# Attention of one layer with V held stationary on column halves, and adaLN units behind the three latent qkv products

## What is computed

```python
q, k, v = qkv_heads(h, wqkv, qn, kn)      # 16 query heads, 4 key/value heads, 64 wide; RMSNorm on q and k
# prompt: every query sees the 128 prompt keys; latent: rope, the 128 latent keys and 128 cached context keys
p = softmax(concat([q @ k.T * 64 ** -0.5, sink]))[..., :-1]
o = einsum('bkgqs,bskd->bqkgd', p, v)      # 4 query heads share one key/value head
return o.reshape(B, L, 1024) @ wo
```

## Time and profile before

| what | value |
|---|---|
| median of 3 runs | 1302.45 us (1299.8 to 1305.2) |
| the profiled execution | 1300.94 us, of which its span (first to last instruction) 1299.0 us |
| mean granted TensorE clock | 0.997 of full speed |
| busy share of the span | PE 98%, DVE 34%, ACT 25%, POOL 4% |
| DMA | 497.42 MB, mean 383 GB/s |
| layer 1: latent and prompt qkv products | 664.5 to 715.2 us |
| layer 1: attention up to the projection's first matmul | 715.2 to 761.0 us |
| layer 1: projection | 761.0 to 788.6 us |

### The profile page before, as it was taken

How to read it: one execution, slowest core, us unless ns; L and a number is a source line. 1 busy time by engine, 2 the same in 40 slices (tenths; PEclk the granted TensorE clock), 3 DMA queues, 4 the chain that set the end, 5 groups by cost and what they waited for, 6 DMA issues and landing times.

```text
span 1299.0 us, 18966 instructions
## 1 busy us (share of the span) xinstructions
PE 1267.8 (98%) x7020; PEld 709.7 (55%) x7020; DVE 440.6 (34%) x1503; ACT 324.4 (25%) x718; POOL 56.8 (4%) x86
## 2 busy tenths in 40 slices
PE   6999999999999999999999899999999999999998
PEld 3876775545545454455454578655445444544544
DVE  1696272222222222222235535422222222222223
ACT  3575331121121122112121433112212211221111
POOL 0295000000000000000000000000000000000000
PEclk9999999999999999999999999999999999999999
DMA  9987999999999999999996557699999999999994
GB/s 365 385 324 302 405 401 403 414 419 419 420 420 421 421 420 421 420 419 421 363 413 284 235 227 292 248 403 418 419 420 420 421 420 421 421 421 421 419 419 193
DMA packets 84022, 497.42 MB, mean 383 GB/s; under 512 B 10681, under 2 KB 19553, under 8 KB 27648
## 3 DMA queue, kind: packets, MB, share of 16 engines
q1 hardware_dynamic: 83392, 496.47, 93.4%
q10 hardware_dynamic: 576, 0.22, 0.1%
HBM read 493.26 MB, written 3.41 MB: 382 GB/s over the span
## 4 chain that ended last, share of the span: by engine, by line
PE 85%; DVE 6%; DMA 6%; ACT 2%; SPq 1%; issue 1%; POOL 0%; DVEq 0%; ACTq 0%
PE ps L951 34%; PE ps L983 17%; PE ps L994 9%; PE ps L922 7%; PE ps L638 4%; DVE ps L1574 3%; PE ps L730 3%; DMA ring<-in_conv_w_dram 2%; PE ps L865 2%; DMA ring<-in_ada_w_dram 2%; DMA S<-in_exp_w_up_dram 2%; PE ps L606 1%; PE ps L969 1%; PE ps L906 1%; PE ps L961 1%; SPq L403 1%
## 5 line engine op out<-in xcount | busy, mean ns | idle before, releaser
L951 PE MATMUL ps<-ring,xg 128*64 128x512 f32 x1344 | 296.8, 593 | 0.2
L951 PEld LDWEIGHTS ps<-ring,xg 128*64 128x64 f32 x1344 | 104.6, 137 | 186.8 <-issue 167.9
L951 PE MATMUL ps<-S,xg 128*64 128x512 f32 x704 | 154.8, 592 | 0.3 <-DMA S<-in_exp_w_up_dram 0.3
L983 PE MATMUL ps<-ring,W 128*64 128x512 f32 x672 | 153.5, 598 | 0.0
L1866 DVE TENSOR_TENSOR ypart<-ps,ypart 128x512 fp32r<-128x512 f32 x128 | 88.5, 691 | 179.8 <-ACT ypart L1396 179.8
L1855 DVE SCALAR_TENSOR_TENSOR vec<-silu_h,W,ps 128x256 f32<-128x256 f32 x64 | 30.8, 481 | 333.3 <-ACT silu_h L1390 333.3
L994 PEld LDWEIGHTS ps<-comb,ypart 128*128 128x128 f32 x1024 | 126.3, 190 | 18.6 <-issue 18.6
L994 PE MATMUL ps<-comb,ypart 128*128 128x256 f32 x1024 | 135.2, 285 | 0.0
L1390 ACT ACTIVATE silu_h<-ps 128x256 f32<-128x256 f32 x64 | 24.6, 385 | 407.3 <-PE ps L951 407.3
L1385 ACT ACTIVATE xg<-ps 128x384 f32<-128x384 f32 x176 | 83.3, 492 | 168.1 <-PE ps L922 168.1
L1396 ACT ACTIVATE ypart<-ps 128x512 fp32r<-128x512 f32 x128 | 76.5, 598 | 184.6 <-PE ps L983 184.6
(11 more groups left out here) (249 smaller groups left out, 1097.4 us busy)
## 6 DMA issues: line engine op xcount, KB each, us to landing
ring<-in_exp_w_gate_dram SPq DMA_DIRECT2D x86, 1024.0 KB, 15.8
ring<-in_exp_w_up_dram SPq DMA_DIRECT2D x86, 1024.0 KB, 18.4
ring<-in_exp_w_down_dram SPq DMA_DIRECT2D x86, 1024.0 KB, 18.2
S<-in_exp_w_gate_dram SPq DMA_DIRECT2D x44, 1024.0 KB, 16.2
S<-in_exp_w_up_dram SPq DMA_DIRECT2D x44, 1024.0 KB, 19.0
S<-in_exp_w_down_dram SPq DMA_DIRECT2D x44, 1024.0 KB, 18.9
ring<-in_ada_w_dram SPq DMA_DIRECT2D x26, 1024.0 KB, 21.2
S<-in_ada_w_dram SPq DMA_DIRECT2D x22, 1024.0 KB, 14.4
```

Source lines behind the costliest of these rows:

```text
L951: mm = pe.matmul(PGU[64 * b:64 * b + 64, :].rearrange("p (h f) -> p h f", h=2), xg[:, places[k][m], 64 * b:64 * b + 64], gate_up_of(w[b])[ ...
L983: mm = pe.matmul(bank[64 * b:64 * b + 64, :], hidT[:, j, 64 * b:64 * b + 64], down_of(w[b])[:, j, n * 512:(n + 1) * 512], start=(j == 0), ...
```

## The change

Three edits, all in layer 1's mixer. (The convolution's taps that run as products with diagonal matrices on PE, `conv_taps`, are in both kernels and the diff leaves them as they are.)

- The eight adaLN units that lay between the latent qkv products run behind the third of them; ACT's and DVE's order follows, and DVE finishes unit group 4 only after the latent norm and rope.
- V is the stationary operand, 64 columns wide, and the transposed probabilities of all four query heads (512 columns) move. The two turns of a pair write the two column halves of one bank, so the result comes out with the head dimension on the partitions, which is what the projection reads. So `otok`, its 16 transposes and the four copies go; `wo` is loaded in another row order by four DMAs. As the queries now lie along the free dimension of the result, the division by the row sum moves ahead of the transposes (`scaled`, on the probabilities in place).
- The order of the attention changes with it: ACT copies the context half of the latent probabilities and the results, DVE the other half; the values of two turns are made together at the end of a pair; the prompt's q and k are transposed ahead of the first turn.

```diff
         B0 = 2 * EW
         qkv = ring_f[:, B0:B0 + 3072].rearrange("p (g n) -> p g n", g=G)
-        otok = ring_f[:, B0 + 3072:B0 + 5120].rearrange("p (g n) -> p g n", g=G)
...
-        probT = W[:, 2816:3840].rearrange("p (b n) -> p b n", b=2)
+        probT = W[:, 2816:4864].rearrange("p (b k n) -> p b k n", b=2, k=2)
+        TURNED = [2 * (i + 1) if i < NKV else NKV + i + 1 for i in range(2 * NKV)]
...
                     sp.wait_ge(at_qkv, 6)
-                    sp.dma_start(wo, attn_wo[0].rearrange("(k p) n -> p k n", p=P)).then_inc(ld_wo, 16)
+                    for j in range(NKV):
+                        b = j % 2
+                        sp.dma_start(wo[HD * b:HD * b + HD, QG * (j // 2):QG * (j // 2 + 1), :],
+                                     attn_wo[0, QG * HD * j:QG * HD * (j + 1), :].rearrange("(q d) n -> d q n", d=HD)
+                                     ).then_inc(ld_wo, 16)
...
-            def project(w, x, ready, per, loaded, banks):
-
-                pe.wait_ge(loaded, 16)
+            def project(w, x, ready, per, loaded, banks, first=1, loads=1):
...
                             if b == h == 0:
-                                pe.wait_ge(ready, k // per + 1)
+                                pe.wait_ge(ready, k // per + first)
...
-                    qkv_product(1, 0)
-                    ada_products(range(EARLY, EARLY + 4), ps[2])
-                    qkv_product(1, 1)
-                    ada_products(range(EARLY + 4, EARLY + 8), ps[2])
-                    qkv_product(1, 2)
+                    for n in range(3):
+                        qkv_product(1, n)
+                    ada_products(range(EARLY, EARLY + 8), ps[2])
+                    qkv_product(0, 0)
                     ada_transposes(4, ps[2])
-                    qkv_product(0, 0)
                     qkv_product(0, 1)
...
                     def at_transposes(i):
                         nk = 1 + HEADS[i][0]
-                        pe.wait_ge(at_exp, i + 1)
-                        if i == 2:
+                        pe.wait_ge(at_on, i + 1)
+                        if i == 0:
                             pe.wait_ge(at_trc, 7)
+                        else:
+                            pe.wait_ge(at_ptc, TURNED[i - 1 if i <= NKV else i - 2])
                         for kk in range(nk):
+                            bank = ps[4 + kk] if nk == 2 else ps[4 + i % 2]
                             for q in range(QG):
-                                mm = pe.transpose(ps[4 + kk][:, q * T:(q + 1) * T],
+                                mm = pe.transpose(bank[:, q * T:(q + 1) * T],
                                                   prob[:, i % 2, q, kk * T:(kk + 1) * T], ident)
                         mm.then_inc(at_pt, 1)
 
-                    def at_values(i):
-                        g, j = HEADS[i]
+                    def at_values(m):
+                        g = HEADS[2 * m][0]
                         nk = 1 + g
-                        pe.wait_ge(at_ptc, i + 1)
-                        if i >= 1:
-                            pe.wait_ge(at_on, i)
-                        for q in range(QG):
-                            for kk in range(nk):
+                        pe.wait_ge(at_ptc, TURNED[2 * m + 1])
+                        if m >= 1:
+                            pe.wait_ge(at_otc, m)
+                        for kk in range(nk):
+                            for b in range(2):
+                                j = HEADS[2 * m + b][1]
                                 v = (qkv[:, g, (NH + NKV + j) * HD:(NH + NKV + j + 1) * HD] if kk == 0
                                      else vctx[:, j * HD:(j + 1) * HD])
-                                mm = pe.matmul(ps[6][:, q * HD:(q + 1) * HD],
-                                               probT[:, kk, q * T:(q + 1) * T], v,
+                                mm = pe.matmul(ps[6][HD * b:HD * b + HD, :], v, probT[:, b, kk, :],
                                                start=(kk == 0), stop=(kk == nk - 1))
                         mm.then_inc(at_o, 1)
...
                     at_scores(0)
+                    qk_transposes(0, [ps[4], ps[5], ps[6]])
                     ada_products(range(EARLY + 9, EARLY + 12), ps[7])
-                    for i in range(G * NKV):
-                        at_transposes(i)
-                        if i % 2 == 0 and i + 2 < G * NKV:
-                            at_scores(i // 2 + 1)
-                        if i % 2 == 1:
-                            ada_products([EARLY + 12 + i // 2], ps[7])
-                        at_values(i)
-                        if i == 1:
-
-                            pe.wait_ge(at_on, 2)
-                            qk_transposes(0, [ps[4], ps[5], ps[6]])
-
-                    pe.wait_ge(at_on, G * NKV)
-                    for b in range(4):
-                        for h in range(2):
-                            for g in range(G):
-                                mm = pe.transpose(
-                                    ps[b][:, (2 * h + g) * T:(2 * h + g + 1) * T],
-                                    otok[:, g, (2 * b + h) * P:(2 * b + h + 1) * P], ident)
-                        mm.then_inc(at_ot, 1)
+                    for m in range(NKV):
+                        at_transposes(2 * m)
+                        if m + 1 < NKV:
+                            at_scores(m + 1)
+                        at_transposes(2 * m + 1)
+                        ada_products([EARLY + 12 + m], ps[7])
+                        at_values(m)
                     ada_transposes(5, ps[7])
-                    project(wo, oT, at_otc, 2, ld_wo, AB)
+                    project(wo, oT, at_otc, 4, ld_wo, AB, 3, NKV)
...
-                    qkv_copies(1, range(2))
+                    qkv_copies(1, range(3))
+                    qk_roots(1, 20, 40)
                     ada_copy(4, ps[2])
-                    qkv_copies(1, range(2, 3))
-                    qk_roots(1, 20, 40)
...
-                    for i in range(G * NKV):
-                        exps(i)
-                        if i == 2:
-                            qk_copies(0, [ps[4], ps[5], ps[6]])
-                    ada_copy(5, ps[7])
-                    for b in range(4):
-                        act.wait_ge(at_ot, b + 1)
-                        act.activation(oT[:, 2 * b:2 * b + 2, :].rearrange("p k t -> p (k t)"), ps[b][:, :],
-                                       ACT.Copy).then_inc(at_otc, 1)
+                    def context_copy(i):
+
+                        act.wait_ge(at_pt, i + 1)
+                        if i >= 2:
+                            act.wait_ge(at_o, i // 2)
+                        act.activation(probT[:, i % 2, 1, :], ps[5][:, :], ACT.Copy).then_inc(at_ptc, 1)
+
+                    def output_copy(m):
+
+                        g, j = HEADS[2 * m]
+                        act.wait_ge(at_o, m + 1)
+                        act.activation(oT[:, 2 * j:2 * j + QG, g * T:(g + 1) * T],
+                                       ps[6][:, :].rearrange("p (q t) -> p q t", q=QG), ACT.Copy).then_inc(at_otc, 1)
+
+                    qk_copies(0, [ps[4], ps[5], ps[6]])
+                    exps(0)
+                    for m in range(NKV):
+                        exps(2 * m + 1)
+                        if m < NKV // 2:
+                            context_copy(2 * m)
+                            context_copy(2 * m + 1)
+                        if m + 1 < NKV:
+                            exps(2 * m + 2)
+                        else:
+                            ada_copy(5, ps[7])
+                        output_copy(m)
...
-                    ada_finish(4, ps[2])
...
                         else:
+                            ada_finish(4, ps[2])
                             dve.wait_ge(at_nrm, 1)
...
-                    def prob_copies(i):
+                    def prob_copy(i):
                         dve.wait_ge(at_pt, i + 1)
-                        for kk in range(1 + HEADS[i][0]):
-                            ins = dve.tensor_copy(probT[:, kk, :], ps[4 + kk][:, :])
-                        ins.then_inc(at_ptc, 1)
-
-                    def outputs(i):
-                        g, j = HEADS[i]
-
-                        step(dve.tensor_tensor(stat[:, 72 + 4 * i:76 + 4 * i], stat[:, 72 + 4 * i:76 + 4 * i],
-                                               stat[:, 112 + 4 * i:116 + 4 * i], ALU.add))
-                        step(dve.reciprocal(stat[:, 72 + 4 * i:76 + 4 * i], stat[:, 72 + 4 * i:76 + 4 * i]))
-                        dve.wait_ge(at_o, i + 1)
-                        dve.tensor_tensor(
-                            otok[:, g, 4 * j * HD:4 * (j + 1) * HD].rearrange("p (h d) -> p h d", h=QG),
-                            ps[6][:, 0:QG * HD].rearrange("p (h d) -> p h d", h=QG),
-                            stat[:, 72 + 4 * i:76 + 4 * i, None].to_broadcast([P, QG, HD]), ALU.mult
-                        ).then_inc(at_on, 1)
+                        if i >= 2:
```

(36 more changed lines are left out.)

## The result

The changed kernel took 1296.06 us (median of five runs, 1293.01 to 1297.62), the kernel before beside it 1301.87: a ratio of 0.9948 [0.9925, 0.9971], 5.8 us faster. The same two, timed again, gave 1293.99 (1292.51 to 1295.29) against 1302.86: 0.9922 [0.9896, 0.9947]. The profiled execution of after lasted 1297.62 us (span 1295.8). It is the slowest of the first five, so its rows show the change near its worst.

The account below looks back on a forecast made before the run. The changed stage was taken as bound by the latency of turns between PE, DVE and ACT. 1.36 + 6.9 - 1.2 = 7.1 us off the profiled 1300.94 gave 1293.8; the median, 1.5 above, 1295.3, range 1291.7 to 1300.0.

Parts of the forecast that it names:

- What bounds the stage, and the block: Layer 1's attention: latency of turns between engines bounds it; everything from the projection on, weight stream included, moves as a block.
- Part 1: adaLN units behind the latent products: 1.17 us of gap and 0.19 of slower products go, 1.36 in all.
- The bound of 1.4: Upper bound on the gain from moving the adaLN units; the lower was 0.9, the gap alone.
- Part 2's path: New attention's chain, first scores at 716.03 to projection at 752.7: 6.9 us of the 8.25 us earlier projection start.
- The division: New division on the probabilities: two short steps and a multiply, 1.65 us a latent turn, 1.1 a prompt turn.
- The values: Products with V held: 1.9 us for a latent pair, 1.0 for a prompt pair.
- The form changes: Rival: matmul form changes around the four values cost eight times 0.19, 1.5 us more, 1296.8; chance 0.13.
- The clock: Thin PE work from 744.3 to 750.3 brings one stretch at 1.20 GHz, costing 1.2 us (0.6 to 1.7).
- the early gap: PE idle 1.8 us before the attention's first transposes; the clock was taken to hold there.
- The step from there to the median: From the profiled execution's 1293.8 us to the runs' median: 1.5 above, as before the change, so 1295.3.
- The slower rival: Clock stays at 1.20 GHz through the whole attention, PE becomes the bound: 1309.7 us; chance 0.05.
- `wo`: Four loads issued at 713.9 cost nothing between the old rate and half of it (4 MB, 20 us).

Follow-up runs that it names:

- The delay before the projection: Late-filled changed kernel with twenty idle matmuls (4.4 us) between the adaLN transposes and the projection: median 1297.61 us.
- before filled: Kernel before with idle matmuls in PE's gaps of the old attention: 1299.79 us, 0.9984 of before.
- part 1 alone: Kernel before plus only the eight adaLN units moved behind the three latent qkv products: 1298.45 us, 0.9969 of before.
- the late fill: Changed kernel plus ten idle matmuls ahead of the last two turns' transposes: 1293.25 us, 0.9929 of before; again 1293.38.
- filling the early gaps: Changed kernel with the late idle matmuls and more in the attention's earlier gaps: 1293.67 us, 0.993 of before.
- without the multiply: Late-filled changed kernel (three and three idle matmuls) without the multiply that divides the probabilities: 1290.78 us, one run.
- part 2 alone: Changed kernel with the adaLN units put back between the latent qkv products: 1297.12 us, 0.9956 of before.

## Why the prediction came out right, and where its terms did not

1295.3 was forecast, 1296.06 measured, and 1293.99 the second time; 1294.00 over all eleven runs. The mechanism (the chain of waits, the block behind it, a late fall of the clock) is borne out; that the number came so near is in part luck, as the sum below shows. Step by step:

**What bounds the stage, and the block.** Right. The chain still goes PE, ACT, DVE in turn, and the delay before the projection came out at the end (4.2 to 4.4 of 4.46). The stream of weights starts 4.0 us sooner. The block is not rigid, though: from the projection's start to the end it is 538.51 and 539.17 for after, 538.21 for before and 537.77 for before filled, and the tail behind DVE's last copy, 0.5 to 0.9 longer with the new attention, is a term that the working did not have.

**Part 1.** 1.36 forecast, 1.43 measured between the two profiles. The bound of 1.4 was too low, though: it took the old wait as 0.89, the one in the trace. That wait was 1.0 and 1.81 in two other profiles with the old order, and the stage 52.99 and 54.01, while the new order has no such wait and took 51.44 or 51.45 in nine profiles. So the step is worth 1.4 to 2.6, by the execution. That part 1 alone gave 3.9 in the medians is more than that; the rest may be the clock of the old attention, which before and part 1 alone share but lose by the execution (1308.39 and 1306.55 at most), but it was not isolated.

**Part 2's path.** 36.67 forecast (716.03 to 752.7), 37.07 measured at full clock: 0.4 short, or 1%. Most waypoints hold to 0.2 once the later start is added (0.95): the first values at 730.01 for 730.05, the third at 746.50 for 746.35, the last transposes at 750.90 for 750.7. The division, which no row of before showed, was sized from a multiply of the same form: 1.65 for a latent turn; in the chain it is 0.17, 0.19 and 1.24, the last against the 1.22 of the earlier trace rows. The values were put at 1.9 and 1.0; rows above have 1.96 and 1.89, and 1.10.

Some 0.3 of the 0.4 is adding and not price. Redone with its own prices, the path ends at 752.98 in place of 752.7: division 0 at 723.75, transposes 1.09 and scores 2.02 make 726.86 and not 726.7; 743.05 and a copy, maxima and a copy (0.65 + 1.25 + 0.65) make 745.6 and not 745.4. And the maxima's 1.79 runs from DVE's start at 719.44; from the scores' end at 719.41 it is 1.82.

**The form changes.** The rival priced eight changes at 0.19, 1.5 us in all. Beyond the forecast, the four values show 0.06, −0.01, 0.10 and 0.01 (the last at full clock, with the late fill): 0.16. The transposes and scores beside them took what they took before (1.09, and 1.95 to 2.00 against 2.02). The Trainium skill, TensorEngine Tiling, Key Properties, has the engine drain when the tiling mode changes; the rows here show no price of that size for it.

**The clock.** The place was right: the clock fell at about 750 in one profile and just before 748 (0.91 in the row from 746) in the other, PE's work there was as thin as forecast (2.65 of 6 us from 745.25 on, for about 2), the early gap kept the clock, and filling the early gaps changed nothing. The price was the mis-sized term. 1.2 (0.6 to 1.7) was forecast; the two profiles have 39.72 and 39.39 against 37.07, so 2.65 and 2.3. The working took 2.9 us of work, part of it slow; the rows have 3.26 at full clock and all of it slow (transposes 0.45 more, unit 0.87, values 0.90, adaLN transposes 0.46). The other half of that step failed too, in the other direction: one slow stretch was counted for every run, and by their mean clocks some eight of eleven seem to have had none of that length. And the same loss on the side of before was taken as the 1.66 of one trace, where it varies from run to run: before filled stayed within 2.0 us in ten runs, before beside it spread over 9.8 in 23.

**The sum.** In the profiles: 7.1 forecast; 0.07 more for part 1, 0.4 less for the path, 1.45 less for the clock and 0.16 less because the old projection started at 760.79 (PE's timeline) rather than 760.95. That is 5.2, where the two stages gave 1.43 + 3.68 = 5.1. The step from there to the median failed as well: the new median was to stand 1.5 above the profiled execution, and stood 1.56 below it the first time (1297.62) and 1.15 below it the second (1295.14). So the profiled execution came out 3.8 slower than the 1293.8 forecast for it and the median 0.8 slower than its own: the two misses cancel in part, which is luck. In the timed runs the gain is 5.8 and 8.9 in the two sessions, on both sides of the forecast; of the 3.1 between them 2.1 lie in the median of after and 1.0 in that of before.

**The slower rival.** Its mechanism exists, but in the old attention: part 1 alone, with 50.00 in its profile, lost 8.2 to it against 41.76 of the filled one. In no profile of the new attention did the slow stretch begin before 746.

**`wo`.** Right at the edge. The four loads ran at half of the old rate, the bound that was given, and landed by about 738, with PE asking at 756.6 in after and at 749.5 at the earliest (without the multiply). No wait for it appears.

## What to carry to other kernels

In a stage bound by turns between engines, the length of a new order can be read from the chain of waits, if each new step is priced from a row of the same form: here to within 0.4 us of 37, on a forecast gain of 6.9. An engine's busy time does not give the price (DVE's 7.7 us of multiplies cost 3.05). A DMA wait or a fall of the clock in the trace is one draw: take its size as a range, on the side of the kernel before too, and look at the scatter and the mean clock of the runs before trusting it. Useful work that can stand in the gaps (units, transposes for a later step) fills them as idle products do and leaves the end of the chain as well: here it took 0.8 us off, half of its own 1.6, because a DVE copy then ended last.

## What the runs showed of the hardware

**Loads into 64 partitions ran at half the rate.** While `wo` came as four loads of 1 MB, each into one half of the partitions, the DMA engines were counted as busy all the time, but moved half as much as usual (4-us stretches of after):

```profile
720.00:724.00 4.00, 2.86 (x26) 0.68 (x24) 3.33 (x12) 4.00 (x18) 0.00 (x0) 1.00 1.03 207
724.00:728.00 4.00, 3.47 (x29) 2.84 (x30) 3.04 (x6) 1.33 (x5) 0.00 (x0) 1.00 1.04 208
728.00:732.00 4.00, 3.51 (x22) 0.98 (x20) 3.79 (x14) 2.63 (x11) 0.00 (x0) 1.00 1.04 204
```

At the same share the old single load into all partitions had 410 GB/s. It was hidden here (PE asked at 756.6), but by these rates it holds back the queue behind it for some 10 us more, an estimate from 4 MB at 207 against 410 GB/s. What makes the rate half, the partitions or the layout of the pieces, was not tried apart.

**The clock's low level can last.** The granted clock stayed at 0.50 for 20 us with PE busy 2.00 of 2 us in the rows of part 1 alone, yet came back after some 7 us in both profiles of after. The row just before its fall in part 1 alone has PE busy for 1.06 of 2 us; part 2 alone kept 1.00 behind a row of 0.43. A single row's busy time did not tell which it would be.
